# Latent rows normed inside the out-projection stage, and two-block experts at equal distances

## The chip, the cores and the metric

The kernel runs on one core of a Trainium2 chip. The metric is device time in microseconds (us) from launch to end. All data are fp32, which TensorE (PE) multiplies in two recorded instructions per matmul call. The weights of the second block's 32 experts come in 384 transfers of 1 MB, each read once.

## What is computed

A first block of four layers works on two streams of 256 tokens with 1024 features, the *latent* and the *context* stream. A second block follows on the latent stream only, with a hybrid mixer and a layer of routed experts. Cut to what the change touches:

```python
for i in range(4):                      # mixers: window attention, latent attention, mLSTM, window attention
    h_l = rmsnorm(x_lat, g_pre) * (1.0 + sc_l) + sh_l          # "norm" and "modulate"
    h_c = rmsnorm(x_ctx, g_pre) * (1.0 + sc_c) + sh_c
    y_l, y_c = mixer(h_l, h_c)          # begins with h @ w_in, ends with o @ w_out
    x_lat = x_lat + gt_l * rmsnorm(y_l, g_post)
    x_ctx = x_ctx + gt_c * rmsnorm(y_c, g_post)                # layers 0 to 2

def routed_moe(h, ...):                 # 256 tokens, 4 of 32 experts each
    logits = h @ w_router + b_router
    top_v, top_e = top_k(logits, 4); gates = softmax(top_v)
    # assignments are sorted by expert into padded blocks; for each block
    #   y = clamped_swiglu(xb @ w1[e] + b1[e]) @ w2[e] + b2[e]
    # and the gated rows are added into their tokens
```

## The kernel before

**Layout and engines.** Activations are held transposed: feature tile `k` (0 to 7) by tokens, columns 0 to 255 latent and 256 to 511 context. `XT` is the residual stream, `HT` the normed and modulated input of a projection, `YT` a projection's gated output, `SQ` squares of it or of `XT` (both in `BIG`), `RMS` and `RSTD` the root and its inverse (in `PW`), `GAIN` the factor of the modulation. PE multiplies, ScalarE (ACT) moves results out of the accumulation banks `PS` (eight of 512 columns), takes roots and squares and modulates, VectorE (DVE) inverts, normes and adds, GpSimd (POOL) adds squares in `add_squares` (L369), and SyncE (SP) issues all transfers. Each engine runs its own queue in the order in which the code is written. Work is written in blocks (`with nc.Block()`), and at a block's end every engine waits for all others.

**Weights of the layers** stream through a ring of three 2 MB slots, in program order; a slot is loaded anew once PE has used it.

**The out-projection stage** (`project_out(l, ...)`, L557) of layers 0 to 2 makes 16 tiles of 128 features by 256 tokens: (0, m) are the latent ones, (1, m) the context ones, m from 0 to 7, 16 recorded matmuls each, in banks 0 to 3 in turn. ACT squares each (L579) and scales it into `YT` (L580); DVE adds the squares up (L599). While the context tiles are multiplied, the latent rows are finished: PE sums the squares over the features after tile (1, 0) (L547), ACT takes the root (L381), DVE inverts (L385) and adds the residual (L390, L391), ACT squares the new `XT` after the eviction of (1, 4) (L356), POOL adds these eight tiles up, PE sums them after (1, 6) (L376), ACT takes the second root and DVE inverts it. DVE then adds the context tiles' squares (L599).

**The in-projection stage** of the next layer (`window_layer`, `latent_layer`, `memory_layer`) begins with `first_tiles`. PE sums the context squares (L424), then makes the latent halves of four tiles one after another, each product waiting for its row of `HT`; between the third and the fourth it waits for POOL and sums the squares of the context residual (L376). Then come the context halves (in the last layer queries are wanted for latent tokens only, so there are none). DVE does, in this order: `GAIN` (L396), norm of the eight latent rows (L404), inverse, residual and inverse of the context rows, their norm. ACT: context root, modulation of the latent rows (L417), context squares, root, modulation of the context rows, and only then the evictions of the tiles. The lines of the products are L985 and L987 in layer 1, L1166 in layer 2, L866 in layer 3; the full-width tiles that follow (512 tokens) are L1003, L1181 and L884.

**The experts.** The rows of an expert are cut into blocks of 64. The weights lie in one buffer of 12 chunks of 1 MB. SP walks through the experts (`loads`), and loads chunk c of the next expert once `used` says that the last block of the present one has used chunk c. PE walks through the blocks: bias (L2364), first products with chunks 0 to 7 (L2372), two small steps, second products with chunks 8 to 11 (L2398). The order of the experts is computed on the chip: expert 0 is always first, and each other expert gets a key, by rank among the experts of one block (`light`) or of more (`heavy`), and the keys are sorted. With H heavy and L light experts the q-th light one has the key (q - 0.5) H, the r-th heavy one (r - 0.75) L.

Of the kernel before, what the change touches and what calls it, by code (L numbers as in the profile page):

```python
# [155 lines left out]
def layers_and_experts_kernel(nc, t, consts_at, out):  # L156
# [3 lines left out]
    with ctx:  # L160
# [232 lines left out]
        def norm_vector(dve, l, g_pre, streams, pending=False, part=0):  # L393

            m = modulation(l)[:, 3 * KT * part:, :]
            dve_chain.link(dve, nc.vector.scalar_tensor_tensor(GAIN[:, :, 0:streams], m[:, KT:2 * KT, :], 1.0,  # L396
                                                               col(g_pre).unsqueeze(2).to_broadcast([P, KT, streams]), ALU.add, ALU.mult))
            for tok in (LATENT, CONTEXT)[:streams]:
                if pending and tok is CONTEXT:
                    inverse(dve, CONTEXT)  # L400
                    residual(dve, CONTEXT)
                    inverse(dve, CONTEXT, 1)
                for k in range(KT):
                    nc.vector.tensor_tensor(HT[:, k, tok], XT[:, k, tok], RSTD[:, tok], ALU.mult).then_inc(S["normed_ready"].sem, 1)  # L404

        def norm_scalar(act, l, streams, pending=False, part=0):
            if pending:
                root(act, PS[:, 6, 0:LAT], CONTEXT)
            for s, tok in enumerate((LATENT, CONTEXT)[:streams]):
                if pending and tok is CONTEXT:  # L410
                    for k in range(KT):
                        act.wait_ge(*at("residual_ready", k + 1))
                        square(act, k, CONTEXT, SQ)
                    root(act, PS[:, 7, 0:LAT], CONTEXT, 1)
                for k in range(KT):
                    act.wait_ge(*at("normed_ready", s * KT + k + 1))
                    nc.scalar.activation(HT[:, k, tok], HT[:, k, tok], ACT.Identity, bias=modulation(l)[:, 3 * KT * part + k, s:s + 1],  # L417
                                         scale=GAIN[:, k, s:s + 1]).then_inc(S["h_ready"].sem, 1)

        def first_tiles(pe, pending, tiles, product):  # L420
# [16 lines left out]
        def norm_passed(streams, pending=False):  # L437
            S["normed_ready"].passed(KT * streams)
            S["h_ready"].passed(KT * streams)
# [86 lines left out]
        def project_out(l, ot, streams):  # L526
# [5 lines left out]
            with nc.Block() as block:  # L532
# [11 lines left out]
                def _(pe):  # L544
# [5 lines left out]
                    for j, (s, m) in enumerate(tiles):  # L550
# [11 lines left out]
                        if (s, m) == (1, 6):  # L562
# [2117 lines left out]
```

## Time and profile before

| | us |
|---|---|
| runs (three) | 2548.09, 2548.47, 2551.39; median 2548.47 |
| the profiled execution, its own time | 2551.05 |
| its span, first to last instruction | 2549.2 |
| layers 0 to 3 and hybrid mixer | to about 1515 |
| experts' blocks, 36 of them | 1521 to 2536 |
| PE busy | 2393.0 (94%) |
| mean granted TensorE clock | 0.971 |

PE is busy nearly throughout, so what counts is where it stands still or is paced by something else: by another engine in the layers, by arriving weights among the experts. In the timeline views a row is a run of equal instructions with its start, its length, engine, source line, operation and count, and in brackets the idle time of that engine before it with what ended it. Rows of PE in such a run overlap by 0.16 us at their ends, so a tile of 16 records (3.62 us) takes 3.45 us when others follow. A granted clock of 1.00 is 2.4 GHz, 0.50 is 1.2 GHz.

### The profile page before, as it was taken

To read this page: it belongs to the slowest core of one execution; us is meant where nothing else is said; L and a number is where in the kernel's file an instruction comes from. 1 tells how busy PE (TensorE), PEld (TensorE's weight loads), DVE (VectorE), ACT (ScalarE), POOL (GpSimd) and SP (SyncE) were. 2 spreads that over 40 slices of the span, in tenths; PEclk is the share of its full clock that TensorE was granted. 3 is DMA by queue.
4 is the path that set the end of the run, shared out by engine and by line. 5 is a ranking of instruction groups with operands and counts; after the bars stand their busy time and mean duration, and the time that the engine had idled before them with its cause. 6 is when DMAs were issued, how large, how long until landed. Compare 5 with 4: busy or idle time off the path is not lost. (4 is left out here: it accounts for less than half of the span.)

```text
span 2549.2 us, 31871 instructions
## 1 busy us (share of the span) xinstructions
PE 2393.0 (94%) x11948; PEld 1284.9 (50%) x11949; DVE 931.9 (37%) x2133; ACT 643.1 (25%) x1480; POOL 46.8 (2%) x57
## 2 busy tenths in 40 slices
PE   6999999999999998899899789999999999999998
PEld 4545685468645567676686553333233323332332
DVE  2107624143610584527354424232223223322333
ACT  3016633243311253326332321111111111111111
POOL 0000000000100000100001000000000000000000
PEclk8999999999999998999999789999999999999999
DMA  8117931200211002339331059699989998999897
GB/s 298 67 66 265 340 120 58 83 34 26 74 66 67 34 1 82 117 112 327 123 133 66 12 200 366 262 418 418 418 345 418 418 418 340 418 418 417 342 418 310
DMA packets 154254, 568.00 MB, mean 223 GB/s; under 512 B 10832, under 2 KB 12368, under 8 KB 121136
## 3 DMA queue, kind: packets, MB, share of 16 engines
q1 hardware_dynamic: 154160, 566.72, 56.9%
q8 instruction: 62, 1.02, 0.2%
q14 instruction: 32, 0.26, 0.0%
HBM read 565.64 MB, written 1.05 MB: 222 GB/s over the span
## 5 line engine op out<-in xcount | busy, mean ns | idle before, releaser
L2372 PE MATMUL PS<-BIG,PW 128*64 128x512 f32 x2304 | 514.9, 598 | 21.6 <-DMA BIG<-in_w 21.4
L2372 PEld LDWEIGHTS PS<-BIG,PW 128*64 128x64 f32 x2304 | 158.5, 137 | 375.5 <-issue 308.9
L2398 PE MATMUL PS<-BIG,PW 128*64 128x512 f32 x1152 | 255.2, 595 | 8.6 <-ACT PW L2475 8.6
L2561 DVE TENSOR_SCALAR PW<-PS 128x512 f32<-128x512 f32 x36 | 24.9, 692 | 528.9 <-PE PS L2372 528.9
L2472 ACT ACTIVATE PW<-PW 128x512 f32<-128x512 f32 x36 | 22.8, 632 | 773.0 <-DVE PW L2561 773.0
L2398 PEld LDWEIGHTS PS<-BIG,PW 128*64 128x64 f32 x1152 | 79.8, 137 | 160.8 <-issue 143.6
L884 PE MATMUL PS<-HT,BIG 128*128 128x512 f32 (+1 forms) x448 | 154.7, 504 | 0.0
L557 PE MATMUL PS<-HT,BIG 128*128 128x256 f32 x640 | 139.5, 379 | 2.1 <-PEq L666 2.1
L557 PEld LDWEIGHTS PS<-HT,BIG 128*128 128x128 f32 x640 | 121.4, 190 | 19.0 <-issue 2.7
L884 PEld LDWEIGHTS PS<-HT,BIG 128*128 128x128 f32 x448 | 86.0, 192 | 62.8 <-issue 56.9
L1183 PE MATMUL PS<-BIG,HT 128*128 128x512 f32 x256 | 110.0, 592 | 0.0
L731 ACT ACTIVATE PW<-PS,ST 128x512 f32<-128x512 f32 (+2 forms) x144 | 84.9, 593 | 16.7 <-DVE ST L776 9.0
L771 DVE TENSOR_REDUCE ST<-PS 128x2 f32<-128x1024 f32 (+2 forms) x72 | 69.9, 971 | 46.4 <-PE PS L1074 39.7
L2581 DVE TENSOR_TENSOR PW<-PS,BIG 128x512 f32<-128x512 f32 x36 | 24.9, 692 | 151.5 <-PE PS L2398 151.5
L1183 PEld LDWEIGHTS PS<-BIG,HT 128*128 128x128 f32 x256 | 48.6, 190 | 61.2 <-issue 61.2
L1722 PE MATMUL PS<-HT,BIG 128*128 128x256 f32 x320 | 72.5, 386 | 4.2 <-ACT HT L417 4.2
L315 PE MATMUL PS<-BIG,COND 128*32 128x256 f32 x1152 | 73.9, 400 | 2.5 <-DVE MOD L337 2.5
L745 ACT COPY PW<-PS 128x512 f32<-128x512 f32 (+2 forms) x144 | 63.5, 490 | 50.4 <-PE PS L689 49.9
L703 PE MATMUL PS<-PW,BIG 128*64 128x128 f32 (+1 forms) x880 | 75.8, 286 | 0.0
L2335 PE MATMUL PS<-BIG,HT 128*64 128x512 f32 x296 | 71.7, 606 | 2.6 <-PEq L2215 2.6
L689 PE MATMUL PS<-CONST,PW 128*128 128x128 f32 x440 | 68.3, 295 | 5.9 <-DVE PW L792 5.8
L2350 PE MATMUL PS<-PW,HT 64*128 64x512 f32 x288 | 71.5, 615 | 0.9 <-DVE PW L2581 0.9
(457 smaller groups left out, 3136.4 us busy)
## 6 DMA issues: line engine op xcount, KB each, us to landing
BIG<-in_w SPq DMA_DIRECT2D x384, 1024.0 KB, 16.8
BIG<-in_l_w_ada SPq DMA_DIRECT2D x24, 2048.0 KB, 8.6
BIG<-in_l_w_in SPq DMA_DIRECT2D x20, 2048.0 KB, 7.9
BIG<-in_w_ada SPq DMA_DIRECT2D x12, 2048.0 KB, 8.0
BIG<-in_l_w_out SPq DMA_DIRECT2D x8, 2048.0 KB, 8.7
BIG<-in_w_in SPq DMA_DIRECT2D x7, 2048.0 KB, 9.0
BIG<-in_w_out SPq DMA_DIRECT2D x2, 2048.0 KB, 8.0
BIG<-in_l_w_in SPq DMA_DIRECT2D x1, 1792.0 KB, 10.9
```

Source lines behind the costliest of these rows:

```text
L315: ins = nc.tensor.matmul(PS[g:g + 32, self.bank, 0:256], COND[:, k, :], w[:, k, half * 256:half * 256 + 256], start=(k < 2), stop=(k >= KT ...
L557: ins = nc.tensor.matmul(PS[:, j % 4, 0:LAT], w[:, k, (m % 4) * P:(m % 4 + 1) * P], ot[:, k, s * LAT:(s + 1) * LAT], start=(k == 0), stop= ...
L703: ins = nc.tensor.matmul(place(heads_at(i)), lhs, turned[:, i % 2, h, j * P:(j + 1) * P], start=(j == 0), stop=(j == len(kts) - 1))
L731: nc.scalar.activation(probs[:, i % 2, h, a:b], PS[:, 2 * (i % 2) + h, a:b], ACT.Exp, bias=nm[:, i % 2, h:h + 1], scale=scale, accum_out=d ...
L771: dve_chain.link(dve, nc.vector.tensor_reduce(mx[:, i % 2, 0:2], s[:, :, a:b], AX, ALU.max))
L884: ins = nc.tensor.matmul(PS[:, j % 4, 0:tok], *ops, start=(k == 0), stop=(k == KT - 1))
L1183: ins = nc.tensor.matmul(o, HT[:, k, m[1] * P:(m[1] + 1) * P], w[:, k, :], start=(k == 0), stop=(k == KT - 1))
L1722: ins = nc.tensor.matmul(o[:, 0:LAT], w[:, k, m % 4 * P:m % 4 * P + P], HT[:, k, 0:LAT], start=(k == 0), stop=(k == KT - 1))
L2335: ins = nc.tensor.matmul(PS[64 * g:64 * g + 64, 6, :], pick[:, a, :], htok[:, a, g * 512:g * 512 + 512], start=(a == 0), stop=(a == 1))
L2350: ins = nc.tensor.matmul(PS[:, 2 * a + g, :], spread[64 * g:64 * g + 64, a * P:(a + 1) * P], ys[64 * g:64 * g + 64, :], start=False, stop= ...
L2372: ins = nc.tensor.matmul(PS[64 * g:64 * g + 64, 4 + half, :], xt[:, c % 4, c // 4, :], W[:, c, half * F + g * 512:half * F + g * 512 + 512 ...
L2398: ins = nc.tensor.matmul(PS[64 * g:64 * g + 64, 7, :], at_[:, k % 4, k // 4, :], W[:, 8 + k // 2, k % 2 * D + g * 512:k % 2 * D + g * 512 ...
```

## The change

In layers 0 to 2 the norm and the modulation of the *latent* rows move from the next layer's in-projection stage into the out-projection stage. DVE does `GAIN` and the eight norms after its second inverse and ahead of the sum of the context squares; ACT modulates four rows after the eviction of tile (1, 5) and four after (1, 6). To make room, ACT's squares go from after (1, 4) to after (1, 2), PE's sum L376 from after (1, 6) to after (1, 4), and the second root from after (1, 6) to after (1, 4). In the in-projection stage DVE and ACT now begin with the context rows, PE waits for no latent row, and in layers 1 and 2 `first_tiles` makes six tiles instead of four (the two more in banks 4 and 5). In layer 1 the sums for the low-rank norms and the first rotation move from after z tile 0 to after z tile 2.

Among the experts the heavy one's key becomes r L and the light one's (q - 0.5)(H + 1).

```diff
+        def norm_gain(dve, l, g_pre, streams, part=0):
...
+        def norm_rows(dve, tok):
+            for k in range(KT):
+                nc.vector.tensor_tensor(HT[:, k, tok], XT[:, k, tok], RSTD[:, tok], ALU.mult).then_inc(S["normed_ready"].sem, 1)
+
+        def modulate_rows(act, l, s, tok, nth=0, part=0, rows=range(KT)):
+            for k in rows:
+                act.wait_ge(*at("normed_ready", nth * KT + k + 1))
...
+        def context_vector(dve):
+            inverse(dve, CONTEXT)
+            residual(dve, CONTEXT)
+            inverse(dve, CONTEXT, 1)
+            norm_rows(dve, CONTEXT)
+
+        def context_scalar(act, l):
+            root(act, PS[:, 6, 0:LAT], CONTEXT)
+            for k in range(KT):
+                act.wait_ge(*at("residual_ready", k + 1))
+                square(act, k, CONTEXT, SQ)
+            root(act, PS[:, 7, 0:LAT], CONTEXT, 1)
+            modulate_rows(act, l, 1, CONTEXT)
...
         def first_tiles(pe, pending, tiles, product):
...
-                            pe.wait_ge(*at("h_ready", s * KT + k + 1))
+                            if not pending:
+                                pe.wait_ge(*at("h_ready", s * KT + k + 1))
+                            elif tok is CONTEXT:
+                                pe.wait_ge(*at("h_ready", k + 1))
...
         def project_out(l, ot, streams):
...
-                        if (s, m) == (1, 6):
+                        if (s, m) == (1, 4):
                             sum_added(pe, LATENT, PS[:, 5, 0:LAT])
...
+                        if (s, m) == (1, 2):
+                            squares()
                         if (s, m) == (1, 4):
-                            squares()
-                        if (s, m) == (1, 6):
                             root(act, PS[:, 5, 0:LAT], LATENT, 1)
+                        if (s, m) in ((1, 5), (1, 6)):
+                            modulate_rows(act, l + 1, 0, LATENT, rows=range(4 * (m - 5), 4 * (m - 4)))
...
                     inverse(dve, LATENT, 1)
                     if beside:
+                        norm_gain(dve, l + 1, f"l{l + 1}_g_pre", 2)
+                        norm_rows(dve, LATENT)
                         sum_tiles(1)
...
-                    first_tiles(pe, True, [(j, 2, done[j]) for j in range(4)], latent_or_context)
+                    first_tiles(pe, True, [(j, 2, done[j]) for j in range(6)], latent_or_context)
...
-                        if kind == "z" and m == 0:
+                        if kind == "z" and m == 2:
                             square_sums()
+                            pe.wait_ge(*at("tile_taken", 6))
                             rope(0)
...
-                    link(nc.vector.tensor_tensor_scan(heavy_rank, ones[:, 0:E], heavy, 0.0, ALU.mult, ALU.add))
+                    link(nc.vector.tensor_tensor_scan(heavy_rank, ones[:, 0:E], heavy, 1.0, ALU.mult, ALU.add))
...
-                    link(ts(tmp, heavy_rank, -0.75, light_rank[:, E - 1:E], ALU.add, ALU.mult))
+                    link(ts(tmp, heavy_rank, -1.0, light_rank[:, E - 1:E], ALU.add, ALU.mult))
```

The order on PE, at the end of layer 0's out-projection and the start of layer 1's in-projection. First before the change (the first row is the eight latent tiles and (1, 0)):

```order
171 L557 MATMUL PS<-HT,BIG 128x256 x72
172 L547 MATMUL PS<-BIG,CONST 128x256
173 L557 MATMUL PS<-HT,BIG 128x256 x48
174 L376 MATMUL PS<-BIG,CONST 128x256
175 L557 MATMUL PS<-HT,BIG 128x256 x8
176 L532 UNCONDITIONAL_BRANCH
177 L966 UNCONDITIONAL_BRANCH
178 L424 MATMUL PS<-BIG,CONST 128x256
179 L985 MATMUL PS<-HT,BIG 128x256 x24
180 L376 MATMUL PS<-BIG,CONST 128x256
181 L987 MATMUL PS<-HT,BIG 64x256 x16
182 L985 MATMUL PS<-HT,BIG 128x256 x24
```

And after it (L574 is the old L557, L438 the old L424, L1014 and L1021 the old L985 and L987, L1018 the two z tiles):

```order
171 L574 MATMUL PS<-HT,BIG 128x256 x72
172 L564 MATMUL PS<-BIG,CONST 128x256
173 L574 MATMUL PS<-HT,BIG 128x256 x32
174 L376 MATMUL PS<-BIG,CONST 128x256
175 L574 MATMUL PS<-HT,BIG 128x256 x24
176 L549 UNCONDITIONAL_BRANCH
177 L995 UNCONDITIONAL_BRANCH
178 L438 MATMUL PS<-BIG,CONST 128x256
179 L1014 MATMUL PS<-HT,BIG 128x256 x24
180 L376 MATMUL PS<-BIG,CONST 128x256
181 L1021 MATMUL PS<-HT,BIG 64x256 x16
182 L1018 MATMUL PS<-HT,BIG 128x256 x16
```

The first L376 stands two tiles earlier; the second still stands behind three latent halves, and three latent halves now follow it (tile 3 and the two new ones) where tile 3 stood alone.

The order on ACT from the eviction of tile (1, 2) to the context squares of the next stage. Before (L579 and L580 evict a tile, L356 are squares, L381 a root, L417 the modulation; the branches are the block's end):

```order
227 L579 ACTIVATE BIG<-PS 128x256
228 L580 ACTIVATE BIG<-PS,GATE 128x256
229 L356 ACTIVATE BIG<-XT 128x256 x8
230 L579 ACTIVATE BIG<-PS 128x256
231 L580 ACTIVATE BIG<-PS,GATE 128x256
232 L579 ACTIVATE BIG<-PS 128x256
233 L580 ACTIVATE BIG<-PS,GATE 128x256
234 L381 ACTIVATE PW<-PS,CONST 128x256
235 L579 ACTIVATE BIG<-PS 128x256
236 L580 ACTIVATE BIG<-PS,GATE 128x256
...
239 L381 ACTIVATE PW<-PS,CONST 128x256
240 L417 ACTIVATE HT<-HT,MOD,GAIN 128x256 x8
```

After (L596 and L597 are the old L579 and L580, L406 the old L417), from the second root on:

```order
230 L381 ACTIVATE PW<-PS,CONST 128x256
231 L596 ACTIVATE BIG<-PS 128x256
232 L597 ACTIVATE BIG<-PS,GATE 128x256
233 L406 ACTIVATE HT<-HT,MOD,GAIN 128x256 x4
234 L596 ACTIVATE BIG<-PS 128x256
235 L597 ACTIVATE BIG<-PS,GATE 128x256
236 L406 ACTIVATE HT<-HT,MOD,GAIN 128x256 x4
237 L596 ACTIVATE BIG<-PS 128x256
238 L597 ACTIVATE BIG<-PS,GATE 128x256
239 L549 UNCONDITIONAL_BRANCH
240 L1063 UNCONDITIONAL_BRANCH
241 L381 ACTIVATE PW<-PS,CONST 128x256
```

The eight modulations moved from behind the block's end to between the evictions of (1, 5), (1, 6) and (1, 7). The order of the experts is made of data, so no instruction moves for it.

## Rows read from the trace of the kernel before

**Rows 1.** Timeline of PE from layer 0's out-projection into layer 1 (columns as told above)

```profile
380.72 3.62 PE L557 MATMUL PS<-HT,BIG 128*128 128x256 f32 x16
386.72 0.67 PE L424 MATMUL PS<-BIG,CONST 128*128 128x256 f32 x2 [2.39 <-PEq L532]
388.45 13.66 PE L985 MATMUL PS<-HT,BIG 128*128 128x256 f32 x48 [1.06 <-ACT HT L417]
402.05 0.70 PE L376 MATMUL PS<-BIG,CONST 128*128 128x256 f32 x2
...
427.77 2.74 PE L979 MATMUL PS<-BIG,CONST 128*128 128x512 f32 x6
...
430.77 29.78 PE L1003 MATMUL PS<-HT,BIG 128*128 128x512 f32 x69
```

**Rows 2.** Timeline of DVE in the same stretch

```profile
383.22 3.19 DVE L599 TENSOR_TENSOR BIG<-BIG 128x256 f32<-128x256 f32 x7
...
386.94 2.77 DVE L404 TENSOR_TENSOR HT<-XT,PW 128x256 f32<-128x256 f32 x8
389.62 1.75 DVE L385 RECIPROCAL PW<-PW 128x256 f32<-128x256 f32 x1
391.41 0.42 DVE L390 TENSOR_TENSOR BIG<-BIG,PW 128x256 f32<-128x256 f32 x1
...
393.80 0.95 DVE L390 TENSOR_TENSOR BIG<-BIG,PW 128x256 f32<-128x256 f32 x1
```

**Rows 3.** Timelines of ACT, then POOL, in the same stretch

```profile
373.78 2.56 ACT L356 ACTIVATE BIG<-XT 128x256 f32<-128x256 f32 x8
...
384.38 0.39 ACT L579 ACTIVATE BIG<-PS 128x256 f32<-128x256 f32 x1 [2.98 <-PE PS L557]
...
387.43 0.47 ACT L381 ACTIVATE PW<-PS,CONST 128x256 f32<-128x256 f32 x1 [2.31 <-PE PS L424]
...
374.58 5.55 POOL L369 TENSOR_TENSOR BIG<-BIG 128x256 f32<-128x256 f32 x7 [373.56 <-ACT BIG L356]
393.61 1.72 POOL L369 TENSOR_TENSOR BIG<-BIG 128x256 f32<-128x256 f32 x2 [13.48 <-ACT BIG L356]
```

**Rows 4.** Stretches: busy us (instructions) of PE, PEld, DVE, ACT, POOL, clock, DMA

```profile
384.40:396.00 11.60, 8.22 (x23) 6.44 (x24) 10.90 (x25) 6.75 (x15) 1.64 (x2) 0.71 0.54 182
660.00:672.00 12.00, 10.72 (x46) 7.83 (x46) 6.95 (x13) 5.79 (x12) 2.54 (x6) 1.00 0.00 0
1421.00:1426.00 5.00, 5.00 (x30) 5.00 (x31) 0.45 (x1) 1.17 (x2) 0.00 (x0) 0.66 0.02 3
```

**Rows 5.** Timeline of PE: layer 2, layer 3, and a stop in the hybrid mixer

```profile
663.86 0.70 PE L376 MATMUL PS<-BIG,CONST 128*128 128x256 f32 x2 [1.28 <-POOL BIG L369]
...
682.36 27.63 PE L1181 MATMUL PS<-HT,BIG 128*128 128x512 f32 x64
...
1055.64 1.13 PE L629 MATMUL PS<-BIG,CONST 128*128 128x256 f32 x4 [3.72 <-ACT BIG L895]
...
1420.99 1.13 PE L2025 MATMUL PS<-BIG 128*128 128x128 f32 x8 [2.39 <-PEq L1930]
```

**Rows 6.** Timeline of PE: starts of experts' blocks, and one wait in a block

```profile
1616.92 1.09 PE L2364 MATMUL PS<-BIG,CONST 1*64 1x512 f32 x8
...
1778.24 1.09 PE L2364 MATMUL PS<-BIG,CONST 1*64 1x512 f32 x8
...
1787.24 1.94 PE L2372 MATMUL PS<-BIG,PW 128*64 128x512 f32 x8 [0.55 <-DMA BIG<-in_w]
...
1869.37 1.09 PE L2364 MATMUL PS<-BIG,CONST 1*64 1x512 f32 x8
...
2508.84 1.09 PE L2364 MATMUL PS<-BIG,CONST 1*64 1x512 f32 x8
```

**Rows 7.** Stretches among the experts, columns as in Rows 4 (the last two: DMA share, GB/s)

```profile
1525.00:1535.00 10.00, 10.00 (x42) 3.03 (x41) 5.26 (x20) 0.00 (x0) 0.00 (x0) 0.86 0.10 14
1593.00:1623.00 30.00, 29.76 (x144) 10.06 (x142) 8.42 (x13) 3.58 (x5) 0.00 (x0) 1.00 0.22 85
```

More of the change, by code:

```diff
@@ L397, in norm_vector @@
                                                                col(g_pre).unsqueeze(2).to_broadcast([P, KT, streams]), ALU.add, ALU.mult))
-            for tok in (LATENT, CONTEXT)[:streams]:
[L399 to L404, printed above, removed]
@@ L406, in norm_scalar @@
-        def norm_scalar(act, l, streams, pending=False, part=0):
-            if pending:
-                root(act, PS[:, 6, 0:LAT], CONTEXT)
-            for s, tok in enumerate((LATENT, CONTEXT)[:streams]):
[L410 to L418, printed above, removed]
+        def norm_rows(dve, tok):
+            for k in range(KT):
+                nc.vector.tensor_tensor(HT[:, k, tok], XT[:, k, tok], RSTD[:, tok], ALU.mult).then_inc(S["normed_ready"].sem, 1)
@@ new lines, in modulate_rows, with norm_vector @@
+        def modulate_rows(act, l, s, tok, nth=0, part=0, rows=range(KT)):
+            for k in rows:
+                act.wait_ge(*at("normed_ready", nth * KT + k + 1))
+                nc.scalar.activation(HT[:, k, tok], HT[:, k, tok], ACT.Identity, bias=modulation(l)[:, 3 * KT * part + k, s:s + 1],
+                                     scale=GAIN[:, k, s:s + 1]).then_inc(S["h_ready"].sem, 1)
+        def norm_vector(dve, l, g_pre, streams, part=0):
+            norm_gain(dve, l, g_pre, streams, part)
+            for tok in (LATENT, CONTEXT)[:streams]:
+                norm_rows(dve, tok)
@@ L985, in latent_or_context @@
                             return nc.tensor.matmul(PS[:, j, t], w[:, k, j * P:(j + 1) * P], HT[:, k, t], start=(k == 0), stop=(k == KT - 1))
+                        if tiles[j][0] == "z":
+                            if k == 0:
+                                ws.wait(pe, tiles[j][2])
+                            return nc.tensor.matmul(PS[:, j, t], ws.view(tiles[j][2])[:, k, (j - 4) * P:(j - 3) * P], HT[:, k, t],
+                                                    start=(k == 0), stop=(k == KT - 1))
                         for half in range(2):
@@ L1165, in latent_or_context @@
                     def latent_or_context(j, k, t):
-                        return nc.tensor.matmul(PS[:, j, t], ws.view(c_in)[:, k, j * P:(j + 1) * P], HT[:, k, t], start=(k == 0),
-                                                stop=(k == KT - 1))
+                        if j == 4 and k == 0:
+                            ws.wait(pe, c_in + 1)
+                        return nc.tensor.matmul(PS[:, j, t], ws.view(c_in + j // 4)[:, k, j % 4 * P:(j % 4 + 1) * P], HT[:, k, t],
+                                                start=(k == 0), stop=(k == KT - 1))
                     ws.wait(pe, c_in)
-                    first_tiles(pe, True, [(j, 2, done[j]) for j in range(4)], latent_or_context)
+                    first_tiles(pe, True, [(j, 2, done[j]) for j in range(6)], latent_or_context)
                     for j, (kind, m, c) in enumerate(tiles):
-                        if j < 4:
+                        if j < 6:
                             continue
```

39 lines of the change are left out of this document (24 added, 15 removed).

## The prediction

> **What bounds the kernel now.** I read three views. First the page: PE is busy for 94% of the span, so the rest of the argument is about the places where it isn't, or is slowed. Second, the timelines around the end of each out-projection. PE ends layer 0's last tile at 380.72 + 3.62 = 384.34 and does nothing until 386.72; it then sums, stops for another 1.06 us until the first latent row is modulated, and takes 13.66 us for three latent tiles [rows 1]. The same 48 instructions would take 3 x 3.45 = 10.36 us at the steady rate. What slows them is the clock: after these stops it was granted at half for part of the stretch, 0.71 in the mean over 11.6 us [rows 4], which is 0.29 x 11.6 x 2 = 6.7 us at 1.2 GHz. Who holds PE: DVE finishes the sum of the context squares at 383.22 + 3.19 = 386.41, and 0.31 us later the next block begins [rows 1, 2]; the norm and ACT's modulation follow. Third, the starts of the experts' blocks. From 1616.92 to 1778.24 there are six blocks without a wait, 161.32 / 6 = 26.89 us each; then three take 91.13 us, 3.5 us more each, and in them PE waits some 0.55 us at each chunk for its transfer [rows 6]. One expert's load takes as long as such a block, 26.89 + 3.5 = 30.4 us. So a one-block expert costs 26.89 us of PE and 30.4 us of transfers, a two-block one 53.8 us and 30.4 us. While PE is in the first block of a two-block expert nothing can be loaded once that expert is complete: from 1593 to 1623 the transfers' share is 0.22 [rows 7], 23 us idle.
>
> **The experts' order.** The pattern in the trace gives the order away: 36 blocks for 32 experts, and four idle stretches of the transfers. The first load starts at about 1534 [rows 7]; two loads later comes the first stop, then after 8, 8 and 8 loads the others, and 5 loads stand behind the last. So experts 2, 10, 18 and 26 in the order have two blocks, H is 4 and L is 28. The old keys give just this: (r - 0.75) 28 = 7, 35, 63, 91 against (q - 0.5) 4 leaves 2, 7, 7, 7 and 5 light ones around them (expert 0 is light and first). The new ones, 28, 56, 84, 112 against (q - 0.5) 5, leave 6, 5, 6, 5 and 6. After each stop the transfers start anew behind PE's use of chunk 0 in the second block, and PE has gained a lead of nearly a buffer: it runs the second block and five light ones unhindered (1616.92 to 1778.24 is this run), and only from the sixth light one on does it wait 3.5 us per block, until the next heavy one's first block included. A stretch of seven costs three waits, of five (the tail) none. The whole is 32 blocks from 1616.92 to 2508.84, 891.92 us, less 32 x 26.89 = 860.5: 31.4 us of waits, three times three blocks.
>
> With the new order a stretch of five costs one wait (the heavy one's first block), of six two, and the tail of six one. Stretches 5, 6, 5 and the tail give 1 + 2 + 1 + 1 = 5 waits. The head must be looked at apart: the first heavy expert is the sixth load. Its eighth chunk would land at 1534 + 5 x 30.4 + 8 x 2.53 = 1706.2, and PE, unhindered from 1616.92 on, begins that block at 1616.92 + 3 x 26.89 = 1697.6 and wants that chunk some 13 us later, 1710.8: 4.6 us of cover, no wait. Of nine waits four go, each 3.3 to 3.5 us, and the tail's one may be a little shorter: 31.4 - 5 x 3.35 = **14.6 us gained**. If the sixth light expert after a stop should wait less than its share, up to 15.6; if the fifth waits partly, as the lead differs by some tenths between stretches, 13.3. No price of the DVE steps changes: the two constants replace constants.
>
> **The latent rows, first in the out-projection.** ACT's squares take 2.56 us [rows 3] and would begin two tiles (6.9 us) earlier, at 366.9. By then DVE is at the residual of row 5; POOL begins at 367.7 (0.8 later, as now) while DVE has five operations left. Where these two ran together after 393.6, DVE's L390 took 0.95 instead of 0.42 us [rows 2] and POOL 1.72 for two, 0.86 each instead of 5.55 / 7 = 0.79 [rows 2, 3]. So DVE ends the residual at about 367.7 + 5 x 0.87 = 372.0, ACT the squares at 372.4, POOL its last addition at 373.6. PE finishes tile (1, 4) at 373.1 and waits 0.5 us instead of the present 0.2: +0.35 us with the handing over. ACT stands in the squares past the end of tile (1, 3), evicts it 3 us late, and nobody waits: the bank is wanted three tiles later. The second root ends at 374.8, the inverse (1.75 us) at 376.6, the first norm row at 377.2, all eight (2.77 us) at 379.6; ACT modulates four rows (0.5 us each) after (1, 5) and four after (1, 6), 2 us in gaps of 2.7 us, which ran idle. So these 5.7 us of DVE and ACT are hidden beside PE's tiles. The sum of the context squares is then done but for its last addition, so the block ends 0.04 + 0.39 (L579) + 0.06 + 0.43 + 0.31 = 1.2 us after PE's last tile instead of 2.4. Net of the 0.35, the next block begins **0.8 us earlier**.
>
> The SBUF — State Buffer page of the Trainium skill (Who interferes with whom) says more harshly that a DVE operation with two SBUF inputs and a GpSimd one exclude each other for a whole instruction. By it five of DVE's and POOL's would alternate at 0.42 + 0.79 = 1.2 us, and the sum would lose 1.3 us in each of the three layers; the trace's 0.87 is what I use.
>
> **Then in the in-projection.** DVE inverts the context root as soon as it is there, 0.71 (387.43 - 386.72) + 0.5 for the root = 1.2 us after the block's start instead of 2.9 (389.62 - 386.72) [rows 1 to 3], so the whole context chain comes 1.7 us earlier: L376 is free at 13.65 us after the start instead of 15.33 (402.05 - 386.72). PE no longer waits for latent rows: its sum and three tiles end 11.0 us after the start. There it meets a **new wait**: 13.65 - 11.0 = 2.65 us for POOL, behind which all remaining tiles are queued. What does this do to the clock? The stop at the start is 1.2 us now; in layer 2 a stop of 1.28 us before 663.86 left it at 1.00 [rows 4, 5]. But after 2.39 us before 1420.99 it was 0.66 over 5 us [rows 4, 5], 3.4 us at half speed, a loss of 1.7. I take this for the new wait, since 2.65 is nearest to it; its bounds are 0 and the 3.35 us that the present stops cost.
>
> Layer 1, from 384.34 to six tiles in both halves: now up to 430.77 and one z tile of 6.87, less the sums of 3.0 us in between (427.77 to 430.77): 434.65, thus 50.3 us. After: 0.35 + 1.2 + 13.65 + 0.6 (L376) + 10.6 (three latent halves; tile 3, made in two parts of 64 features, is taken at 3.65) + 1.7 (clock) + 20.9 (six context halves) = 49.0. Behind L376 the root (0.5), an inverse (1.75) and the first norm and modulation (some 1 us) make the context rows ready about 4 us after it starts, so 10.6 us of latent work hide them. **1.3 us gained.** The sums, put off to after z tile 2, are not wanted before z tile 7 is done, over 30 us later.
> Layer 2: its L376 starts at 663.86 [rows 5], 17.7 us after PE's last tile if the start runs as in layer 1 (402.05 - 384.34), hence at 646.15; now from there to 682.36 + 2 x 6.87 = 696.1, 49.9 us; after 0.35 + 1.2 + 13.65 + 0.6 + 10.4 + 1.7 + 20.7 = 48.6. **1.3 us.**
> Layer 3 has no context halves of queries; PE stops until ACT, busy with the context rows, evicts its tiles (3.72 us before 1055.64 [rows 5]). It goes on when ACT does, 0.8 + 1.7 = **2.5 us** earlier; the lost clock hides in that stop.
> Layers together 5.1 us; bounds: with no loss of clock 8.5, with the present one 1.8, with no earlier end of the block 2.4 less than each.
>
> **Sum.** 14.6 + 5.1 = 19.7 us. The profiled execution takes 2551.05, and would take 2531.4. It lies 2.58 above the median 2548.47, which I carry over: **2528.8 us**.
>
> **Rivals.** (a) The new stop doesn't lower the clock, for it follows 10 us of dense work, while the stop at 1420.99 came behind small matmuls. Layers 1 and 2 give 1.7 more each: 2525.4. For it: 1.28 us didn't. (b) The layers give almost nothing: POOL and DVE exclude each other for whole instructions (3 x 1.3 = 3.9 less), or the clock falls for as long as now (3.3 less): 2532.5. Against: the 0.95 us of L390. (c) The order of the experts stays, because the constants don't do what they say, or the transfers' lead is smaller than the trace shows and stretches of five wait as often as seven: only the layers' 5.1 us, 2543.4. Against: the old keys reproduce the order exactly. (d) Slower: the chain in the out-projection stage comes too late. ACT, queued before (1, 6) and (1, 7) behind a norm that waits for POOL, then evicts after PE's end and the block's end moves out. This decides as soon as the second root comes more than 3 us after 374.8. If POOL's and DVE's exclusion made one addition 2.4 us (three times the 0.79), the root came 11 us late, 8 us per layer beyond the slack: 24 - 19.7, 2552.8. Nothing in the rows shows more than 0.95.
>
> **How the numbers follow.** Mine 0.57, (a) 0.25, (b) 0.12, (c) 0.03, (d) 0.03. The likeliest is 2528.8. The range reaches from (a) less 1 us for the upper bound of the experts' term to (b) plus 1.3 for its lower one: 2524.4 to 2533.8. A measurement of this kernel tells about 0.2% (5.1 us) from no change, so faster is 2543.4 or less: my case, (a), (b), 0.94; (c) lies on the line and counts as the same, 0.03; (d) 0.03.
>
> **What would show it.** In the changed profile: block starts 26.89 us apart but for five intervals of 30 us or more, in the first blocks of experts 12, 18, 19, 25 and 31 (the first in the order is 0); the last block ends about 14.6 us nearer to the first. In the layers: L376 in the out-projection with a stop of about 0.5 us; 1.2 us of idle before L438; no idle before the latent tiles; about 2.7 us before the second L376 and a clock at half behind it; L629 in layer 3 still behind a stop of ACT's. Wrong would be: waits in other blocks than these, no stop at the second L376, or evictions late enough to hold PE in the out-projection.

## The result and the profile after

| | before | after |
|---|---|---|
| median of the runs, us | 2549.55 (2548.09 to 2551.39, 4 runs) | 2526.65 (2525.53 to 2528.63, 4 runs) |
| ratio, with 95% interval | | 0.9911 [0.9893, 0.9928] |
| the profiled execution, own time; span | 2551.05; 2549.2 | 2526.59; 2524.5 |
| PE busy; mean granted clock | 2393.0; 0.971 | 2375.5; 0.976 |

The kernel is 22.9 us faster. Forecast were 19.7 us and 2528.8 us, within 2524.4 to 2533.8. Line numbers have shifted: L564 and L574 are the old L547 and L557, L438 is the old L424, L596 and L597 evict a tile (L579, L580), L401 is a norm (L404), L406 a modulation (L417), L618 the old L599, L1014, L1021 and L1018 the first tiles of layer 1, L1037 its full-width tiles, L1203 and L1218 those of layer 2, L889 and L652 the old L866 and L629; among the experts L2401, L2409, L2387 are the old L2364, L2372, L2350.

The timeline of PE from layer 0 into layer 1, answering to [rows 1] (start, length, line, idle time before it and what ended it):

```profile
373.05 0.70 PE L376 MATMUL PS<-BIG,CONST 128*128 128x256 f32 x2 [0.47 <-POOL BIG L369]
373.58 10.52 PE L574 MATMUL PS<-HT,BIG 128*128 128x256 f32 x48
385.38 0.67 PE L438 MATMUL PS<-BIG,CONST 128*128 128x256 f32 x2 [1.27 <-PEq L549]
385.88 10.52 PE L1014 MATMUL PS<-HT,BIG 128*128 128x256 f32 x48
399.01 0.70 PE L376 MATMUL PS<-BIG,CONST 128*128 128x256 f32 x2 [2.60 <-POOL BIG L369]
399.64 5.35 PE L1021 MATMUL PS<-HT,BIG 128*64 128x256 f32 x32
...
422.38 3.67 PE L1021 MATMUL PS<-HT,BIG 128*64 128x256 f32 x32
...
433.00 7.03 PE L1037 MATMUL PS<-HT,BIG 128*128 128x512 f32 x16
```

The three tiles behind the block's start now take 10.52 us instead of 13.66, without a stop ahead of them. The new stop of 2.60 us stands where it was forecast, and behind it the clock fell: the two-part tile took 5.35 us, and the same matmuls for the context half 3.67 us, a loss of 1.68.

DVE, then ACT and POOL in the same stretch, answering to [rows 2] and [rows 3]:

```profile
367.15 1.00 DVE L391 TENSOR_TENSOR XT<-BIG,XT 128x256 f32<-128x256 f32 x1
368.07 0.95 DVE L390 TENSOR_TENSOR BIG<-BIG,PW 128x256 f32<-128x256 f32 x1
369.05 0.83 DVE L391 TENSOR_TENSOR XT<-BIG,XT 128x256 f32<-128x256 f32 x1
...
376.29 2.77 DVE L401 TENSOR_TENSOR HT<-XT,PW 128x256 f32<-128x256 f32 x8
...
384.63 0.42 DVE L618 TENSOR_TENSOR BIG<-BIG 128x256 f32<-128x256 f32 x1 [2.94 <-ACT BIG L596]
386.59 1.75 DVE L385 RECIPROCAL PW<-PW 128x256 f32<-128x256 f32 x1 [1.53 <-ACT PW L381]
```

```profile
371.97 0.36 ACT L596 ACTIVATE BIG<-PS 128x256 f32<-128x256 f32 x1
...
377.87 2.07 ACT L406 ACTIVATE HT<-HT,MOD,GAIN 128x256 f32<-128x256 f32 x4
...
381.33 2.07 ACT L406 ACTIVATE HT<-HT,MOD,GAIN 128x256 f32<-128x256 f32 x4
```

```profile
367.14 5.85 POOL L369 TENSOR_TENSOR BIG<-BIG 128x256 f32<-128x256 f32 x7 [366.12 <-ACT BIG L356]
```

Five operations of DVE ran slowly beside POOL; the eight norms and eight modulations lie between evictions, and DVE's last addition ends at 385.05, 0.33 us ahead of the next block's sum.

PE in layers 2 and 3, answering to [rows 5], and stretches (busy us and instructions of PE, PEld, DVE, ACT, POOL; then clock, DMA share, GB/s), answering to [rows 4]: behind the start of layer 1, behind its stop of 2.60, and behind that of layer 2:

```profile
659.74 0.70 PE L376 MATMUL PS<-BIG,CONST 128*128 128x256 f32 x2 [2.60 <-POOL BIG L369]
660.28 31.24 PE L1203 MATMUL PS<-HT,BIG 128*128 128x256 f32 x144
691.36 13.90 PE L1218 MATMUL PS<-HT,BIG 128*128 128x512 f32 x32
...
1025.25 0.67 PE L438 MATMUL PS<-BIG,CONST 128*128 128x256 f32 x2 [1.27 <-PEq L549]
...
1038.88 0.70 PE L376 MATMUL PS<-BIG,CONST 128*128 128x256 f32 x2 [2.60 <-POOL BIG L369]
...
1046.73 1.13 PE L652 MATMUL PS<-BIG,CONST 128*128 128x256 f32 x4 [3.70 <-ACT BIG L921]
```

```profile
384.40:396.00 11.60, 10.62 (x49) 9.41 (x50) 9.56 (x17) 3.52 (x10) 3.51 (x5) 1.00 0.53 182
399.60:411.60 12.00, 12.00 (x64) 8.85 (x64) 4.52 (x9) 4.52 (x9) 0.00 (x0) 0.86 0.00 0
660.30:672.30 12.00, 12.00 (x57) 10.58 (x56) 4.52 (x9) 4.51 (x9) 0.24 (x3) 1.00 0.00 0
```

The same stop, behind the same tiles, left the clock at 1.00 in layer 2: nine latent and context tiles took 31.24 us, 3.45 each.

PE among the experts, answering to [rows 6] (starts of blocks around expert 12, one wait inside, and the last block):

```profile
1850.20 1.09 PE L2401 MATMUL PS<-BIG,CONST 1*64 1x512 f32 x8
...
1877.09 1.09 PE L2401 MATMUL PS<-BIG,CONST 1*64 1x512 f32 x8
...
1885.62 1.94 PE L2409 MATMUL PS<-BIG,PW 128*64 128x512 f32 x8 [0.42 <-DMA BIG<-in_w]
...
1906.91 1.09 PE L2401 MATMUL PS<-BIG,CONST 1*64 1x512 f32 x8
...
2481.13 1.09 PE L2401 MATMUL PS<-BIG,CONST 1*64 1x512 f32 x8
...
2511.96 1.99 PE L2387 MATMUL PS<-PW,HT 64*128 64x512 f32 x8 [0.89 <-DVE PW L2618]
```

From the third block on, starts are 26.89 us apart but for 29.82 (expert 12, the rows above), 29.93 (18), 30.43 (19) and 29.88 (25). The last block, expert 31's, is the fifth one: from its start to the last L2387 it takes 30.83 us, where before it took 27.84 (2536.68 less 2508.84). Excess: 2.93 + 3.04 + 3.54 + 2.99 + 2.99 = 15.5 us, against 31.4 before.

**Where the 24.7 us between the spans come from.** Read as the distance of the same point in both traces: 0.5 us ahead of layer 0's out-projection stage, which no edit touches; 1.1 in layer 1 (six tiles done at 433.00 instead of 434.65, less the 0.5); 3.1 in layer 2 (696.1 to 691.36, less 1.6); 1.6 up to layer 3, in a stretch at the start of layer 2's out-projection where 144 records took 32.90 us before and run at the steady rate now; 2.5 at layer 3's start (1055.64 to 1046.73, less 6.4). At the second block (1559.37 and 1550.67) it is 8.7 us; the experts add 16.0.

### The profile page after: what moved, and what is told of

The parts are those of the page before. It is cut to its first block and busy times, and to the rows that moved or that the text cites. A ratio compares the mean times of both kernels' runs of the same rounds, so it can differ in the third digit from the quotient of the medians.

```text
span 2524.5 us, 31998 instructions
## 1 busy us (share of the span) xinstructions
PE 2375.5 (94%) x12012; PEld 1293.8 (51%) x12013; DVE 939.1 (37%) x2133; ACT 641.7 (25%) x1480; POOL 47.8 (2%) x57
## 5 line engine op out<-in xcount | busy, mean ns | idle before, releaser
L2409 PE MATMUL PS<-BIG,PW 128*64 128x512 f32 x2304 | 509.6, 597 | 10.9 <-DMA BIG<-in_w 10.9
L2409 PEld LDWEIGHTS PS<-BIG,PW 128*64 128x64 f32 x2304 | 160.8, 137 | 357.3 <-issue 323.9
L2509 ACT ACTIVATE PW<-PW 128x512 f32<-128x512 f32 x36 | 22.7, 630 | 757.0 <-DVE PW L2598 757.0
L907 PE MATMUL PS<-HT,BIG 128*128 128x512 f32 (+1 forms) x448 | 154.9, 504 | 0.0
L574 PE MATMUL PS<-HT,BIG 128*128 128x256 f32 x640 | 139.5, 379 | 2.1 <-PEq L689 2.1
L574 PEld LDWEIGHTS PS<-HT,BIG 128*128 128x128 f32 x640 | 121.4, 190 | 19.1 <-issue 2.7
L907 PEld LDWEIGHTS PS<-HT,BIG 128*128 128x128 f32 x448 | 86.1, 192 | 62.9 <-issue 56.9
L2372 PE MATMUL PS<-BIG,HT 128*64 128x512 f32 x296 | 71.7, 606 | 2.6 <-PEq L2252 2.6
L2387 PE MATMUL PS<-PW,HT 64*128 64x512 f32 x288 | 71.5, 615 | 0.9 <-DVE PW L2618 0.9
```

Of the source, the lines that this page charges most:

```text
L574: ins = nc.tensor.matmul(PS[:, j % 4, 0:LAT], w[:, k, (m % 4) * P:(m % 4 + 1) * P], ot[:, k, s * LAT:(s + 1) * LAT], start=(k == 0), stop= ...
L907: ins = nc.tensor.matmul(PS[:, j % 4, 0:tok], *ops, start=(k == 0), stop=(k == KT - 1))
L2372: ins = nc.tensor.matmul(PS[64 * g:64 * g + 64, 6, :], pick[:, a, :], htok[:, a, g * 512:g * 512 + 512], start=(a == 0), stop=(a == 1))
L2387: ins = nc.tensor.matmul(PS[:, 2 * a + g, :], spread[64 * g:64 * g + 64, a * P:(a + 1) * P], ys[64 * g:64 * g + 64, :], start=False, stop= ...
L2409: ins = nc.tensor.matmul(PS[64 * g:64 * g + 64, 4 + half, :], xt[:, c % 4, c // 4, :], W[:, c, half * F + g * 512:half * F + g * 512 + 512 ...
```

## The experiments

Runs of one set are compared with runs of the kernel before on the same chip: its medians were 2548.29 us (17 runs) beside the first four, 2549.38 (13) beside the next four and 2548.32 (9) beside the last two. No experiment changes what is computed. Only e8's set, e5 to e8, has the changed kernel beside it. Where a kernel of another set is compared with the changed one, the chips differ; what comes out when each kernel is taken against the kernel before on its own chip (22.7 to 22.9 us less for the changed kernel) is given beside it.

**Each part alone.** e1_order_only is the kernel before with the new keys; e2_rows_only is the changed kernel with the old ones.

```diff
-tensor_tensor_scan(heavy_rank, ones[:, 0:E], heavy, 0.0, ALU.mult, ALU.add)
+tensor_tensor_scan(heavy_rank, ones[:, 0:E], heavy, 1.0, ALU.mult, ALU.add)
...
-ts(tmp, heavy_rank, -0.75, light_rank[:, E - 1:E], ALU.add, ALU.mult)
+ts(tmp, heavy_rank, -1.0, light_rank[:, E - 1:E], ALU.add, ALU.mult)
```

> The kernel before with only the new keys of the experts' order. If a one-block expert's wait for its transfers is what the order saves, the number of waits in blocks goes from nine to five, and with 3.0 us for a first wait after a run of unhindered blocks and 3.5 for a following one the sum goes from 31.5 to 15.5 us: 16 us faster than before, about 0.9937. If the two parts lean on each other (an earlier start of the experts' stage that only the latent rows bring), less than 14. If the gain of the change were mostly the clock's in the layers, under 10.

Measured: 2534.93 us (2530.66 to 2537.24, 6 runs), ratio 0.9945 [0.9933, 0.9957]: 13.4 us, the interval reaching from 11.0 to 17.1. Its trace has five waits, 2.87, 3.02, 3.54, 3.40 and 3.03, 15.9 in all, in experts 12, 18, 19, 25 and 31, and the old stops in the layers.

> The changed kernel with the old keys of the experts' order: only the latent rows are moved. By the prediction's terms 5 to 8.5 us faster than before: 1.3 to 3.0 in layers 1 and 2 each, by whether the clock falls behind the new stop, 2.5 in layer 3, ratio 0.9980 to 0.9967. If the 1.6 us that the changed profile shows between layers 2 and 3 come with the change, up to 10 us. If nearly all of the gain is the experts' order: under 3 us. The block starts of the experts' stage are those of before.

Measured: 2542.05 us (2539.01 to 2547.06, 12 runs), ratio 0.9977 [0.9969, 0.9986]: 6.2 us. Nine waits again, 30.8 us in all. Stops of 1.27 and 2.60 us stand in all three layers, but the clock fell behind none of the 2.60s. Behind layer 1's:

```profile
398.90:410.90 12.00, 12.00 (x72) 9.57 (x72) 4.53 (x9) 4.52 (x9) 0.00 (x0) 1.00 0.01 1
```

The two parts add up to 13.4 + 6.2 = 19.6 us, against 22.7 to 22.9 for both on their own chips. The intervals are some 3 us wide to either side for e1 and 2 for e2, so the sum agrees within them; they show no sign that one part takes from the other, and couldn't show an effect of 2 or 3 us.

**The two more half tiles.** e3_four_tiles makes four tiles in halves, as the kernel before.

```diff
-first_tiles(pe, True, [(j, 2, done[j]) for j in range(6)], latent_or_context)
+first_tiles(pe, True, [(j, 2, done[j]) for j in range(4)], latent_or_context)
```

> The changed kernel, but layers 1 and 2 make four tiles in halves ahead of the others, as before, instead of six. After the sum for which PE waits (L376) one latent half of 3.45 us is left, and the context rows are ready 4.0 us after that sum starts: by that PE stops some 0.5 us once more in each of the two layers and is paced by ACT's modulation (0.5 us a row against 0.43) for another 0.5: about 1 to 2 us slower than the changed kernel, not to be told from it by the time alone. If the two more tiles are what makes the change pay in these layers, 5 us or more slower.

Measured: 2527.12 us (2523.65 to 2527.59, 5 runs), ratio 0.9912 [0.9899, 0.9924], not to be told from the changed kernel. After L376 the fourth latent half, 5.26 us in layer 1 of this trace with the clock down and 3.67 without, covers nearly all that the context rows still need. The context halves start without idle time; behind them PE is paced by ACT's modulation, in layer 2 for 0.7 us (the five halves behind L376 took 18.11 us instead of 5 x 3.45 + 0.16 = 17.41) and in layer 1 for 0.1 (10.63 instead of 10.52). So the change's two more tiles bring 0.8 us in these traces, less than the medians can show.

**The stop of 2.60 us.** e4_sum_later puts PE's second sum ahead of the fifth latent half instead of the fourth, in layers 1 and 2; e10_sum_earlier ahead of the third. The number of tiles is the same.

```diff
-if pending and tok is LATENT and j == 3:
+if pending and tok is LATENT and j == (4 if len(tiles) > 4 else 3):    # e4
...
+if pending and tok is LATENT and j == (2 if len(tiles) > 4 else 3):    # e10
```

> The changed kernel, but in layers 1 and 2 PE sums the squares of the context residual (L376) ahead of the fifth latent half instead of the fourth. The fourth half, 3.45 to 3.65 us, covers the stop of 2.60 us, and the context rows are ready some 18.6 us after the block's start, while PE has latent work up to 22. If that stop costs its length and sometimes the clock behind it: 5.2 us faster than the changed kernel and up to 3.4 more where the clock fell; the granted clock is 1.00 in the first 20 us of layers 1 and 2. If the stop costs only where the chain behind it is late anyway (PE catches up later), no difference.

Measured: 2519.2 us (2519.03 to 2520.36, 4 runs), ratio 0.9888 [0.9873, 0.9902]: 7.4 us below the changed kernel's median on another chip, 6.2 to 6.4 with each against the kernel before on its own. PE in layer 1:

```profile
384.39 10.52 PE L1014 MATMUL PS<-HT,BIG 128*128 128x256 f32 x48
394.85 3.67 PE L1021 MATMUL PS<-HT,BIG 128*64 128x256 f32 x32
398.45 0.70 PE L376 MATMUL PS<-BIG,CONST 128*128 128x256 f32 x2
398.99 7.07 PE L1018 MATMUL PS<-HT,BIG 128*128 128x256 f32 x32
```

No idle time, in layer 2 neither, and the clock does not fall. Two stops are 5.2 us; the rest, 1 to 2 us, is about one fall of the clock.

> The changed kernel with the second sum of squares ahead of the third latent half in layers 1 and 2 instead of the fourth. It isn't ready earlier, 13.6 us after the stage's first sum, so PE's stop there grows from 2.60 to 6.05 us in both layers, and the half that then follows it takes its 3.45 us behind it: 6.9 us slower. My theory adds the clock: a stop of 6.05 us lets it fall every time, 1.7 us in each of the two layers, where the one of 2.60 let it fall in 5 of 12 traced: 2 us more, so 2526.6 + 9 = 2535.6 us, with the clock below 0.90 in the 12 us behind both stops. Rival: the fall hangs on something else than the length of the stop, and comes as often as now: 2533.5 us.

Measured: 2536.77 us (2535.22 to 2539.12, 6 runs), ratio 0.9959 [0.9946, 0.9972]: 10.1 us above the changed kernel's median on another chip, 11.1 to 11.3 with each against the kernel before on its own. PE in layer 1, and the 12 us behind the stop in layer 1 and in layer 2:

```profile
384.50 7.07 PE L1014 MATMUL PS<-HT,BIG 128*128 128x256 f32 x32
397.63 1.22 PE L376 MATMUL PS<-BIG,CONST 128*128 128x256 f32 x2 [6.05 <-POOL BIG L369]
398.64 5.04 PE L1014 MATMUL PS<-HT,BIG 128*128 128x256 f32 x16
```

```profile
398.20:410.20 12.00, 12.00 (x64) 9.08 (x63) 4.53 (x9) 4.52 (x9) 0.00 (x0) 0.86 0.00 0
662.60:674.60 12.00, 12.00 (x45) 10.10 (x44) 4.52 (x9) 4.51 (x9) 0.24 (x3) 0.79 0.00 0
```

The stop is 6.05 us in both layers, as worked out, and the clock fell behind both, by 0.14 x 12 = 1.7 and 0.21 x 12 = 2.5 us. That it falls every time after such a stop is supported by two cases of two, no more.

**Chance or place.** e8_after_again is the changed kernel once more, with no edit.

> The changed kernel as it is, on the same chip as the others of this set. It should take 2525 to 2529 us as before. The stop of 2.60 us before the second sum of squares stands in layers 1, 2 and 3 again. If the clock's fall behind it in layer 1 is a property of the place, the granted clock in the 12 us behind it is 0.86 in layer 1 and 1.00 in layer 2 once more; if it is chance, layer 1 may show 1.00.

Measured: 2526.66 us (2524.76 to 2528.49, 4 runs), ratio 0.9908 [0.9892, 0.9925]. Behind the stops of 2.60 us in layers 1 and 2:

```profile
400.10:412.10 12.00, 12.00 (x64) 8.94 (x64) 4.53 (x9) 4.51 (x9) 0.00 (x0) 0.86 0.00 0
660.80:672.80 12.00, 12.00 (x51) 10.35 (x50) 4.52 (x9) 4.51 (x9) 0.24 (x3) 0.89 0.00 0
```

The fall isn't fixed by the place: with the same kernel it came in layer 2 here and not in the first trace. Over the six traced kernels with this stop in both layers (after, e2, e3, e5, e6, e8) it came in layer 1 in four and in layer 2 in one: 5 of 12. Layer 3 has the same stop, behind the same 10.52 us, in nine traces (after, e2 to e8 and e10), and only in e8's was the tile behind it slow, 5.30 us instead of 3.62; together 6 of 21. Whether the place makes the fall likelier, four of six in layer 1 against two of 15, these traces don't decide.

**What makes an order of experts cheap.** Both are the changed kernel with other keys: e5_long_head puts the one-block experts 6, 7, 7, 7, 1 around the two-block ones (expert 0 counted in the 6), e6_adjacent 14, 0, 0, 0, 14. Both scan from 0.0.

```diff
-ts(tmp, heavy_rank, -1.0, light_rank[:, E - 1:E], ALU.add, ALU.mult)
+ts(tmp, heavy_rank, -0.1, light_rank[:, E - 1:E], ALU.add, ALU.mult)    # e5
...
+ts(tmp, heavy_rank, 1.0, 53.2, ALU.mult, ALU.add)                       # e6
```

> The changed kernel with other constants in the keys of the experts (scan from 0.0, heavy key (r - 0.1) L), so that the one-block experts stand 6, 7, 7, 7, 1 around the four two-block ones. My theory: only the number of blocks that wait counts. The head of six waits nowhere, each stretch of seven costs three waits, the last expert none: nine waits of 3.5 us, 31 us in all, as with the old keys, so 16 us more than the changed kernel's 2526.6 us (the pause of the transfers at the first two-block expert comes as late as in the changed kernel, and that is of no use). Rival: what the new keys save is the early pause of the transfers, which came behind the second expert and now comes behind the sixth, since by then the buffer's lead is used; then this kernel keeps most of the gain and takes about 2530 us.

Measured: 2543.07 us (2539.45 to 2545.78, 10 runs), ratio 0.9973 [0.9964, 0.9983]. Nine waits, 30.9 us: experts 12, 13, 14, then 20 to 22, then 28 to 30; the last block takes 27.84 us, without one. 16.4 us more than the changed kernel, on the same chip. The later first pause of the transfers is worth nothing; the number of waiting blocks is.

> The changed kernel with the four two-block experts one behind another: 14 one-block ones, then the four, then 14. My theory: PE's lead can't grow beyond one buffer, so three of the four two-block experts give nothing. The head of 14 has 4.6 us of cover at expert 6, so expert 8 waits some 2.4 us and 9 to 14 wait 3.5 each; behind the last two-block expert five run free and nine wait: 2.4 + 15 x 3.5 = 55 us of waits against 15.5, 40 us more than the changed kernel: about 2566 us. Rival: only the number of two-block experts ahead counts (each banks 23 us for later): then 23 us of waits in the head and none behind it, 2534 us.

Measured: 2571.99 us (2567.81 to 2573.15, 4 runs), ratio 1.0082 [1.0066, 1.0099], 45.3 us more than the changed kernel. 17 blocks wait, 27.1 us in the head and 31.5 us in the tail (nine times 3.5, as worked out; the second to fourth two-block experts give nothing). The rival, 2534, is out. But my head is 3.6 us short: expert 7 waits already, 2.56 us, and expert 8 3.30. The transfers' share (the figure before the last) in three stretches of this trace shows why:

```profile
1525.00:1575.00 50.00, 48.03 (x250) 20.85 (x248) 20.71 (x40) 6.32 (x9) 0.00 (x0) 1.00 0.94 385
1575.00:1585.00 10.00, 9.76 (x54) 3.47 (x50) 4.24 (x7) 2.36 (x3) 0.00 (x0) 1.00 0.84 311
1585.00:1700.00 115.00, 114.04 (x554) 38.57 (x548) 33.94 (x53) 14.30 (x20) 0.00 (x0) 1.00 1.02 418
```

Between 1575 and 1585 they carried 311 GB/s instead of 418, which is 10 x (1 - 311 / 418) = 2.6 us less of transfers. That is when expert 1 uses chunks 8 to 11 (its second products run from 1577.43 to 1584.52): the load for expert 2, whose last transfer SP had issued by 1585.07, had caught up with PE and waited for those chunks to come free. The head's cover at expert 6 is not 4.6 us but 3.53 - 2.56 = 1.0; of the 3.6 us between them this pause explains 2.6, and the last us stays open.

**Onwards in layer 3.** e7_evict_first is e4 with ACT evicting layer 3's first three tiles between the context rows' second root and their modulation. e9_rotations_later is e7 with PE's second sum behind the fourth latent tile there and each rotation's sum one tile later.

```diff
             root(act, PS[:, 7, 0:LAT], CONTEXT, 1)
+            if beside:
+                beside()                      # e7: evicts tiles 0 to 2 of layer 3
             modulate_rows(act, l, 1, CONTEXT)
...
-                        if 1 <= j <= len(roped):
-                            rope(j - 1)
+                        first_rope = 2 if pending else 1                    # e9
+                        if first_rope <= j < len(roped) + first_rope:
+                            rope(j - first_rope)
```

> The kernel of e4_sum_later (2519.2 us), and in layer 3 ACT evicts the first three tiles between the second root of the context rows and their modulation, in the 2.3 us in which it waited for the inverse and the first norm. My theory: PE's stop of 3.70 us before its first sum of a rotation goes; DVE, busy with the norms until 2.0 us behind that, then turns out as the next to be waited for, at the third rotation, so that 2.3 us of the 3.7 remain as gain: about 2517 us, with one stop of 1 to 2 us for DVE in place of the 3.70. Rival: the modulation of the context rows comes 1.2 us later, and the full-width tiles behind wait for it: nothing gained, 2519.2.

Measured: 2516.72 us (2514.84 to 2518.77, 4 runs), ratio 0.9874 [0.9857, 0.989]. PE in layer 3 (L440, L654 and L909 are L438, L652 and L907 of the changed kernel):

```profile
1019.34 0.67 PE L440 MATMUL PS<-BIG,CONST 128*128 128x256 f32 x2 [1.27 <-PEq L551]
...
1036.97 1.03 PE L654 MATMUL PS<-BIG,CONST 128*128 128x256 f32 x4
1039.26 0.67 PE L654 MATMUL PS<-BIG,CONST 128*128 128x256 f32 x2 [1.27 <-DVE BIG L660]
1039.77 3.62 PE L909 MATMUL PS<-HT,BIG 128*128 128x256 f32 x16
```

The stop of 3.70 for ACT is gone and one of 1.27 for DVE has come, 2.4 us net, as the trace of e4 let me work out. The traces show more than that. Behind the stop of 3.70 the clock fell, and behind the one of 1.27 it didn't (the 12 us behind the stop, first in e4, then in e7):

```profile
1037.80:1049.80 12.00, 11.71 (x45) 9.75 (x46) 5.04 (x13) 1.56 (x5) 0.00 (x0) 0.86 0.31 118
1039.80:1051.80 12.00, 12.00 (x57) 10.58 (x56) 4.91 (x14) 2.13 (x6) 0.00 (x0) 1.00 0.39 150
```

From the stage's first sum to its first full-width tile e4 took 40.60 us (1016.36 to 1056.96) and e7 35.97 (1019.34 to 1055.31): 4.6 us gained in this pair of traces, of which 2.7 are idle time and the rest clock. The medians, of different chips, differ by 2.5, or by 3.6 with each against the kernel before on its own; both are within the spread of e7's runs, 3.9 us.

> The kernel of e7_evict_first (2516.7 us), and in layer 3 PE sums the squares of the context residual behind the fourth latent tile instead of ahead of it, and sums each rotation one tile later. My theory: the stop of 2.60 us ahead of the sum goes, as in layers 1 and 2 of e4_sum_later; the fifth tile then waits only for the eviction of the first, behind ACT's second root, about 1 us, and starts some 16.2 us after the stage's first sum instead of 20.4: 4 us gained, 2512.7 us. Rival: DVE's context chain, 0.9 us later, is what the stage ends on: the stop moves to the rotations or the first full-width tile, and less than 1 us is gained, 2516.

Measured: 2514.17 us (2513.12 to 2516.11, 4 runs), ratio 0.9869 [0.985, 0.9888], the fastest kernel of this study, 12.5 us below the changed one, or 11.3 to 11.5 with each against the kernel before on its own chip.

```profile
1019.43 0.67 PE L440 MATMUL PS<-BIG,CONST 128*128 128x256 f32 x2 [1.27 <-PEq L553]
1019.94 13.98 PE L893 MATMUL PS<-HT,BIG 128*128 128x256 f32 x64
1033.75 0.59 PE L376 MATMUL PS<-BIG,CONST 128*128 128x256 f32 x2
1035.18 1.13 PE L656 MATMUL PS<-BIG,CONST 128*128 128x256 f32 x4 [0.84 <-ACT BIG L924]
1036.15 3.62 PE L911 MATMUL PS<-HT,BIG 128*128 128x256 f32 x16
```

The fifth tile starts 16.7 us behind L440 instead of 20.4, with 0.84 us of idle time left for ACT: 3.7 us, of which 3.3 are left at the first full-width tile (32.66 us behind L440 instead of 35.97). The medians show 2.55, or 1.5 with each against the kernel before on its own chip, less than their spreads. The two profiled spans are equal, 2511.9 and 2512.0, since in the profiled run of e9 some 1.8 us were lost between layer 3 and the experts' third block, and 1.2 in their five waits (17.5 us against 16.3), in places that the edit doesn't touch; what made these losses stays open. So e9's gain over e7 is shown in this stage of the traces, and not by the times.

## Why the prediction was right, step by step

- **The nine waits and the five.** Right in number and place: experts 12, 18, 19, 25 and 31, first blocks. e1 shows it without the other part, e2 and e5 that nine waits cost the same wherever the transfers pause.
- **Their size, 14.6 us.** In the two profiled runs it was 16.0, 1.4 more. There four of the five waits that stay are the first of a stretch and took 2.93 to 3.04 us, and only the second in its stretch took the full 3.54; I had taken 3.35 for each. But this pair is at the ends of what the traces show. The first wait of a stretch lay between 2.87 and 3.6 us in the other traces with this order, and the stretch from the experts' third block to the end of the last L2387 took 932.6 to 934.7 us in the eight traces with it, 933.6 in the mean, where this pair's trace is the shortest. In the three traces with nine waits (before, e2, e5) it took 948.6, 948.0 and 948.0, and before is the longest. The means differ by 14.6 us, the forecast's number; that they agree to the tenth is luck, since single traces differ by 2 us.
- **The head's cover, 4.6 us.** The conclusion (no wait at expert 6) was right, the number wrong: e6 shows 1.0. The step took the loads to run on without a break from 1534, whereas the second of them, expert 2's, stood still for 2.6 us until expert 1 had used its last chunks. Another us of cover is missing for which no run shows a cause. With 1.0 us less of it the first two-block expert would have waited too.
- **Beside the out-projection.** Right: L376 stops for 0.47 us (0.5 forecast), DVE's five operations took 0.83 to 1.00 us (0.87), POOL's seven 5.85, 0.84 each (0.86). The second root ends at 374.26 (374.8 forecast) and the eight norms at 379.06 (379.6), both on time, since this trace runs 0.5 us ahead from before the stage on. Tile (1, 3) is evicted late, at 371.97, and nobody waits. The Trainium skill (SBUF — State Buffer, Who interferes with whom) calls the ports that DVE and GpSimd share an exclusive lock. Held for a whole instruction it would make the two alternate at 0.42 + 0.79 = 1.2 us; the longest operation here took 1.00, so this trace doesn't bear it out.
- **The next block 0.8 us earlier.** Right: idle time before L438 is 1.27 us (1.2) instead of 2.39.
- **The new stop.** 2.60 us against 2.65, and in layer 3 ACT's eviction ended the stop before L652 2.5 us earlier, as forecast. That a lost clock hides in that stop e8 shows: its tile behind the 2.60 us took 1.68 us longer, and the stop for ACT was 2.01 us instead of 3.70.
- **The clock behind it, 1.7 us in each of layers 1 and 2.** The size held where it fell (1.68 us in the rows of L1021), the certainty didn't: 5 of 12. The term was 3.4 us for both layers, and at 5 of 12 it would be 1.4 in the mean, an estimate. So the forecast and rival (a) were both half right. In the profiled run the fall came in layer 1 alone: 1.1 us gained there (1.3 forecast) and 3.1 in layer 2 (1.3 forecast), the difference being one fall.
- **The carry-over of 2.58 us.** The profiled run of before lay high, that of after at its median. Against the median of before, 2549.55, the forecast of 19.7 us lacks 3.2: 1.4 for the waits and 1.8 for the clock that held in layer 2. The 2.1 us between the traces that no edit made (0.5 and 1.6 above) are about the profiled run's distance from the median. Over all traces the account is 14.6 for the waits and 5.1 + 2.0 for the layers, 21.7 us, an estimate a us below the 22.7 and 22.9 of the two sets; of the terms the clock's was then the one mis-sized.
- **The rivals.** (b), exclusion or the old loss of clock, is out by DVE's 0.83 to 1.00 us; (c) by e1; (d) by the root, on time at 374.26, and by evictions that held PE nowhere in that stage.

What the prediction didn't ask is whether the new stop could be avoided. It named the 2.65 us and placed one latent half ahead of the sum too few. e4 shows that moving one call by one tile was worth 6.2 to 7.4 us, no less than the whole move of the latent rows (6.2).

## What to carry to other kernels

When work that fed an engine is taken out of a chain, work out when the next link of the chain arrives, and put as much independent work ahead of that wait as the engine can do until then; a wait placed one tile too early stalls all that is queued behind it, and may cost clock besides. Where a stream of transfers can't keep up with short units and idles during long ones, count the units beyond what one buffer of lead covers: what counts is the longest stretches, not when the pauses fall, and the first unit of each that waits often does so only in part. Two profiled executions can differ by a us or two in places that no edit touches, so line them up point by point before the difference is given to a cause.

## What the hardware showed that I had not expected

A stop of 2.60 us in dense work, the same to 0.01 us and behind the same 10.52 us of tiles, let the granted clock fall in 5 of 12 cases in layers 1 and 2, and in one of nine in layer 3; where it fell, the work behind took 1.3 to 1.7 us longer. A stop of 6.05 us let it fall in both cases, one of 1.27 us in none of the traces of layers 1 to 3 of the kernels with the change. The stop of 3.70 us in layer 3, which stands one tile behind the one of 2.60, was followed by a clock of 0.86 over 12 us in all seven traces that have it (after, e2 to e6, e10). What decides at 2.60 us isn't shown. And while DVE and POOL both worked on the buffers, each DVE operation rose from 0.42 to 0.83 to 1.00 us while POOL's hardly changed (seven took 5.85 us, against 5.55 [rows 3], where DVE did not work beside it): the loss is on DVE's side.
